# First feed-forward's norm root applied behind PSUM, norm sums in the gap, late latent work of block one spread

## The reference

```python
def first_block(x, ...):
    xn = rmsnorm(x, norm_mix_g)
    # MLA attention (8 heads) over latents of rank 384 and 256, differential attention (4 heads)
    q = rmsnorm(q_lat, mla_q_norm_g) @ mla_w_uq      # 64 plain and 32 rotated columns per head
    kv = rmsnorm(kv_lat, mla_kv_norm_g) @ mla_w_ukv  # keys (uk) and values (uv)
    x = x + merged @ w_out
    hn = rmsnorm(x, norm_ffn_g)                      # the norm that is moved
    hid = silu(hn @ w_ffn_gate) * (hn @ w_ffn_up)
    x = x + hid @ w_ffn_down
    return rmsnorm(x, norm_final_g)

def second_block(x, c, ...):                         # ada: mod = silu(c) @ ada_w + ada_b
    x = x + 0.5 * gate0 * swiglu(modulate(x, norm_g[0], shift0, scale0), ffn1...)
    x = x + gate1 * hybrid_mixer(modulate(x, norm_g[1], shift1, scale1), ...)
    x = x + 0.5 * gate2 * swiglu(modulate(x, norm_g[2], shift2, scale2), ffn2...)
    return x
```

## Time and profile before

| | |
|---|---|
| median of 3 runs | 1987.5 us (1986.34 to 1988.85) |
| profiled execution: time, span | 1989.44 us, 1987.8 us |
| PE busy | 1948.9 us, 98% |
| DVE, ACT, POOL busy | 1007.3, 724.4, 57.6 us |
| mean granted TensorE clock | 0.996 of full speed |

### The profile page before, as it was taken

One profiled execution on the slowest core, in us unless ns is written; L12 is line 12 of the kernel. 1 busy time (PEld: TensorE's weight loads), 2 busy tenths in 40 slices (PEclk: granted clock), 3 DMA queues, 4 the chain that ended last, 5 costly groups with the idle time before them and its releaser, 6 DMA issues.

```text
span 1987.8 us, 25472 instructions
## 1 busy us (share of the span) xinstructions
PE 1948.9 (98%) x9196; PEld 1577.2 (79%) x9200; DVE 1007.3 (51%) x1572; ACT 724.4 (36%) x1225; POOL 57.6 (3%) x95
## 2 busy tenths in 40 slices
PE   9998999999999999999999999999999999999999
PEld 6776777877888888788888887867778878888887
DVE  6757335656655554643334335867834653333322
ACT  5455344432222222422322324445545442223221
POOL 0001000001111000000000001000000000000000
PEclk9999999999999999999999999999999999999999
DMA  5211212227667554333333332211111323333332
GB/s 175 75 64 54 64 54 75 86 73 238 208 216 220 175 191 126 106 107 100 95 95 98 104 106 75 76 64 43 43 54 44 101 69 107 101 97 96 96 106 95
DMA packets 57521, 207.22 MB, mean 104 GB/s; under 512 B 6448, under 2 KB 6576, under 8 KB 57440
## 3 DMA queue, kind: packets, MB, share of 16 engines
q1 hardware_dynamic: 46800, 167.68, 27.0%
q0 software_dynamic: 10640, 38.44, 6.2%
HBM read 203.96 MB, written 2.10 MB: 104 GB/s over the span
## 4 chain that ended last, share of the span: by engine, by line
PE 89%; DVE 5%; ACT 3%; issue 2%; DMA 1%; DVEq 0%; SPq 0%; ACTq 0%; POOLq 0%
PE PS L426 25%; PE PS L428 25%; PE PS L427 25%; PE PS L920 2%; PE PS L889 1%; PE PS L904 1%; DVE Y L1591 1%; DMA ADA<-ada 1%; PE PS L682 1%; ACT HI L1073 1%; PE PS L876 1%; DVE LO L1488 1%; DVE BIAS L1866 1%; PE PS L448 1%; ACT XH L1122 1%
## 5 line engine op out<-in xcount | busy, mean ns | idle before, releaser
L1488 DVE TENSOR_TENSOR LO<-RAW,HI 128x1024 fp32r<-128x1024 f32 x311 | 380.7, 1225 | 462.1 <-ACT HI L1073 461.0
L426 PE MATMUL PS<-XH,HI 128*128 128x512 f32 x1472 | 593.2, 403 | 9.1 <-DVE GATE_1M L1934 3.5
L428 PE MATMUL PS<-XH,LO 128*128 128x512 f32 x1472 | 575.7, 391 | 0.0
L427 PE MATMUL PS<-XL,HI 128*128 128x512 f32 x1472 | 574.9, 391 | 0.0
L1073 ACT ACTIVATE HI<-RAW 128x1024 fp32r<-128x1024 f32 x311 | 328.5, 1058 | 597.5 <-PE PS L428 591.4
L426 PEld LDWEIGHTS PS<-XH,HI 128*128 128x128 f32 x1472 | 277.4, 188 | 77.3 <-issue 20.9
L428 PEld LDWEIGHTS PS<-XH,LO 128*128 128x128 f32 x1472 | 277.0, 188 | 59.2
L427 PEld LDWEIGHTS PS<-XL,HI 128*128 128x128 f32 x1472 | 277.9, 189 | 50.8
L426 PE MATMUL PS<-HIDH,HI 128*128 128x512 f32 x528 | 206.3, 391 | 0.0
L427 PE MATMUL PS<-HIDL,HI 128*128 128x512 f32 x528 | 206.1, 390 | 0.0
L428 PE MATMUL PS<-HIDH,LO 128*128 128x512 f32 x528 | 206.1, 390 | 0.0
(11 more groups left out here) (364 smaller groups left out, 2145.0 us busy)
## 6 DMA issues: line engine op xcount, KB each, us to landing
RAW<-weights SPq DMA_DIRECT2D x311, 512.0 KB, 3.6
ADA<-ada POOLq DMA_DIRECT2D x72, 512.0 KB, 4.6
X<-x_in SPq DMA_DIRECT2D x4, 512.0 KB, 7.4
y_out<-X SPq DMA_DIRECT2D x8, 256.0 KB, 4.5
SQC<-squares SPq DMA_DIRECT2D x1, 320.0 KB, 9.7
TAB_P<-positions POOLq DMA_DIRECT2D x1, 256.0 KB, 4.8
POS<-positions POOLq DMA_DIRECT2D x1, 256.0 KB, 3.5
LAMS<-lambdas POOLq DMA_DIRECT2D x1, 128.0 KB, 5.4
```

Source lines behind the costliest of these rows:

```text
L426: mm(bank, a, moving[0][:, t, :], start=start, stop=False)
L427: mm(bank, a, moving[1][:, t, :], start=False, stop=False)
L428: ins = mm(bank, z, moving[0][:, t, :], start=False, stop=stop)
L1488: V.tensor_tensor(LO[n0 % 3][:], RAW[n0 % 3][:], HI[n0 % 3][:].bitcast(F32), ALU.subtract)\
```

## The change

Four things are changed.

**Norm 3.** ACT and DVE make `XH` and `XL` out of x and the gain alone (`gained`, `gained_lo`), tile by tile during `out_proj(0)`. `behind` starts at once after `out_proj`; the norm's sums stand behind its third tile, the spread behind its sixth. The roots are copied to `R0`. DVE multiplies each gate bank by `R0` (`scale_gate`) before ACT's Silu, which now waits for `gate_scaled`; the up bank stays unscaled, and the down product is multiplied by `R0` before it is added to x.

**Norms 4, 5, 6.** `first_sums` leaves the last product and opens the gap; tile 6's square is added by DVE, so that it sums `RB[:, 0]` (and `SUM_G` for norm 4) only. The last tile of x is added in two halves of 256 tokens, and each half is squared by itself. `WARM` has one or two idle matmuls less in its first place.

**Late latent work.** `piece_step` puts the query product uq0 from step 10 to 11 and uq2 from 11 to 12, KR is rotated at step 11 instead of 13, the placing of queries is divided, and DVE makes half of the key copies (`nope_keys`) that ACT made.

**POOL.** The two memsets of `QF` and `KF` wait for the last product's chunks instead of the last addition to x.

```diff
-WARM = [None, None, None, (2, 1, 1), (2, 2, 1), (2, 1, 1), (2, 1, 1)]
+WARM = [None, None, None, (1, 1, 1), (0, 2, 1), (1, 1, 1), (1, 1, 1)]
...
-    return 2 + p if p < 5 else 7 + (p - 5) // 2 if p < 15 else p - 3
+    return 2 + p if p < 5 else 7 + (p - 5) // 2 if p < 12 else 5 + p // 2 if p < 16 else p - 3
...
-    pool.wait_ge(sem("x_added"), 3 * DT)
+    pool.wait_ge(sem("chunk_used"), FIRST["down2"] + 3 * DT - 2)
     pool.memset(QF[64:66, :, :], 1.0).then_inc(sem("f_ones"), 1)
+    pool.wait_ge(sem("chunk_used"), FIRST["down2"] + 3 * DT - 1)
     pool.memset(KF[64:66, :, :], 1.0).then_inc(sem("f_ones"), 1)
...
+        first_sums(k)
...
-        pe.wait_ge(sem("squared"), NTB[k + 1] - 1)
-        for n, src in enumerate((RB[:, 0, :], SQ[:, 0, :])):
+        for b in range(NB):
+            mm(PS[:, 7, 8 + b:9 + b], RB[:, 0, b * P:(b + 1) * P], SQV["ones"][:, 0:1],
+               start=b == 0, stop=False)
+        if k == 4:
+            pe.wait_ge(sem("g_sum_added"), DT)
             for b in range(NB):
...
-            pe.wait_ge(sem("g_squared"), DT - 1)
-            pe.wait_ge(sem("g_sum_added"), DT - 1)
...
-        pe.wait_ge(sem("squared"), NTB[k + 1])
         for b in range(NB):
+            if b == 0:
...
+            if k == 3 and t == 2:
+                first_sums(3)
+                last_sums(3)
+            if k == 3 and t == 5:
+                norm_spread(3)
...
-            sums = {5: lambda: first_sums((3, 6)[b])} if m == DT - 1 else {}
-            used(split_product(PS[:, m % 4, :], w, range(8), range(8), (mh, ml), between=sums))
+            used(split_product(PS[:, m % 4, :], w, range(8), range(8), (mh, ml)))
...
-        all_released()
+        if f:
+            all_released()
+        else:
+
+            pe.wait_ge(sem("x_added"), XA["out1"] + 6)
...
                 if isinstance(i, int) and i == 0 and j == 0:
                     behind(k, n0, (0, 1))
+                    if f == 0:
+                        all_released()
...
-    norm(3)
...
+        A(SQ[:, 1, 0:S // 2], X[:, nt - 1, 0:S // 2], ACT.Square).then_inc(sem("half_squared"), 1)
+        act.wait_ge(sem("x_added"), XA[AHEAD[k]] + DT)
+        A(SQ[:, 1, S // 2:S], X[:, nt - 1, S // 2:S], ACT.Square).then_inc(sem("squared"), 1)
...
+        if k == 3:
+            return
...
-            for m in range(2 * (p - 18), 2 * (p - 18) + 2):
...
+            m = 2 * (p - 18)
+            act.wait_ge(sem("uk_done"), m + 1)
...
+                if b == 0:
+                    gained(m - 1)
...
+    def gained(t):
+
+        A(XH[:, t, :], X[:, t, :], ACT.Copy, scale=col("g_ffn", t)).then_inc(sem("split_hi"), 1)
...
-                act.wait_ge(sem("chunk_used"), 6 * i + (n0 + 2 * j + 1))
-                A(SILU[j], PS[:, 2 * j, :], ACT.Silu).then_inc(sem("silu"), 1)
+                if f == 0:
+                    act.wait_ge(sem("gate_scaled"), 3 * i + (j + 1))
+                    A(SILU[j], SILU[j], ACT.Silu).then_inc(sem("silu"), 1)
...
+        if k == 3:
+            V.tensor_copy(R0[:], PS[:, 6, :]).then_inc(sem("normed"), 1)
+            v.wait_ge(sem("normed"), NDB[4])
+            return
...
+                .then_inc(sem("q_rotated"), 1)
+
+    def nope_keys(m):
...
+            v.wait_ge(sem("uk_done"), m + 1)
+        for r in range(2):
+            h = 2 * m + r
+            V.tensor_copy(KM[h // 4][0:64, h % 4, :], PS[64 * r:64 * r + 64, latent_bank(f"uk{m}"), :])\
+                .then_inc(sem(LATENT_FREE[f"uk{m}"][0] if r else "key_placed"), 1)
...
-            if s == 13:
+            if s == 11:
                 rotate_shared_keys()
-            if s in (14, 15):
-                rotate_queries(s - 14)
+            if s == 14:
+                turn_queries(0)
+            if s == 15:
+                place_queries(0, range(4))
+            if s in (15, 16):
+                nope_keys(2 * (s - 15) + 1)
...
+            if a == 1 and u == 0:
+                turn_queries(1)
+            if a == 1 and 1 <= u < 3:
+                place_queries(1, range(2 * u - 2, 2 * u))
+            if a == 1 and u == 3:
+                v.wait_ge(sem("q_rotated"), 8)
...
+            if m:
+                add_square(k, m - 1)
+                if b == 0:
+                    gained_lo(m - 1)
...
+            for part in parts(m):
+                x, y = X[:, m, part], PS[:, m % 4, part]
+                if b == 0:
+                    ins = V.tensor_tensor(x, x, y, ALU.add)
...
+    def parts(m):
+
+        return (slice(0, S // 2), slice(S // 2, S)) if m == DT - 1 else (slice(0, S),)
...
+                if f == 0:
+                    scale_gate(i, j)
...
+        def scale_gate(i, j):
+
+            v.wait_ge(sem("chunk_used"), 6 * i + (n0 + 2 * j + 1))
+            V.tensor_tensor(SILU[j], PS[:, 2 * j, :], R0[:], ALU.mult).then_inc(sem("gate_scaled"), 1)
...
+                if f < 2 and not (isinstance(i, int) and (i, j) == (0, 0)):
+                    add_square(4 + f, j - 1, i)
+                    if f == 0:
+                        add_square_g(j - 1, i)
...
+                for part in parts(2 * i + j) if f < 2 and isinstance(i, int) else (slice(0, S),):
+                    y = PS[:, 2 + j:3 + j, part]
+                    x = X[:, bass.ds(2 * i + j, 1), part]
+                    if f == 0:
+                        V.tensor_tensor(T[:, 1:2, part], y, R0[:, part].unsqueeze(1), ALU.mult)\
+                            .then_inc(sem("down_scaled"), 1)
+                        if isinstance(i, int):
+                            v.wait_ge(sem("down_scaled"), 2 * i + j + 1 + (part.stop == S and 2 * i + j == 7))
+                        else:
+                            v.wait_ge(sem("down_scaled"), 2 * i + (j + 1))
+                        ins = V.tensor_tensor(x, x, T[:, 1:2, part], ALU.add)
```

More of the change, by code:

```diff
@@ L888, in attention @@
                             pe.wait_ge(sem("v_copied"), 2 * NB + u + 1)
+                        if a == 1 and u == 4 * NB:
+                            pe.wait_ge(sem("q_rotated"), 8)
+                            pe.wait_ge(sem("k_shared"), 8)
                         mm(PS[:, u % 3, 0:n], at_["q"](h, i), at_["k"](h, n), start=True, stop=False)
@@ L997, in two @@
                                 pe.wait_ge(sem("hid_lo"), FT * f + 8 * g + blocks)
-                            sums = {}
-                            if f < 2 and isinstance(i, int) and (i, j, g) == (3, 1, 1):
-                                sums[4] = lambda: first_sums(4 + f)
                             used(split_product(PS[:, 2 + j, :], w, range(blocks), range(8 * g, 8 * g + blocks),
-                                               (HIDH, HIDL), first=g == 0, last=g == 2, between=sums))
+                                               (HIDH, HIDL), first=g == 0, last=g == 2))
                 two(0)
@@ L1123, in high, with norm @@
                         .then_inc(sem("split_hi"), 1)
-            def norm(k, first=0):
+            def norm(k):
                 nt, src, width, g, oh, ol = NORMS[k]
-                for t in range(first, nt):
-                    square(k, t)
+                act.wait_ge(sem("x_half"), k - 2)
+                act.wait_ge(sem("sum_added"), SAB[k] + nt - 2)
+                A(SQ[:, 1, 0:S // 2], X[:, nt - 1, 0:S // 2], ACT.Square).then_inc(sem("half_squared"), 1)
+                act.wait_ge(sem("x_added"), XA[AHEAD[k]] + DT)
+                A(SQ[:, 1, S // 2:S], X[:, nt - 1, S // 2:S], ACT.Square).then_inc(sem("squared"), 1)
                 stds(k)
@@ L1361, in attention @@
                         k = u - 4
+                        if k == 0:
+                            act.wait_ge(sem("q_rotated"), 8)
                         if k:
@@ L1386, in out_proj @@
                         square(k, m - 1)
+                        if b == 0:
+                            gained(m - 1)
                 load_roots()
-                act.wait_ge(sem("x_added"), XA[f"out{b + 1}"] + DT)
-                norm(k, first=DT - 1)
+                if b == 0:
+                    act.wait_ge(sem("x_added"), XA["out1"] + DT)
+                    gained(DT - 1)
+                norm(k)
+            def gained(t):
+                A(XH[:, t, :], X[:, t, :], ACT.Copy, scale=col("g_ffn", t)).then_inc(sem("split_hi"), 1)
             def ffn(f):
@@ L1440, in ffn @@
                     load_roots()
-                    act.wait_ge(sem("x_added"), XA[f"down{f + 1}"] + DT)
-                    norm(4 + f, first=DT - 1)
+                    norm(4 + f)
             act.wait_ge(sem("eps_set"), 1)
@@ L2096, in two @@
                                 .then_inc(sem("g_last"), 1)
-                        if f < 2 and not (isinstance(i, int) and (i, j) in ((0, 0), (3, 1))):
-                            add_square(4 + f, j - 1, i)
-                            if f == 0:
-                                add_square_g(j - 1, i)
                 two(0)
```

86 lines of the change are left out of this document (43 added, 43 removed).

## The result

The changed kernel takes 1972.4 us (median of four runs, 1969.0 to 1974.0) against 1988.2 us: ratio 0.9916, interval 0.9900 to 0.9933, a gain of 15.8 us where 19.6 were forecast. Two later sets of the same kernel gave 0.9915 (0.9902 to 0.9929) and 0.9901 (0.9887 to 0.9916), 1971.9 and 1969.4 us.

A forecast was written before the change was run, and what follows sets the result against it. PE, busy 98% of the span, was taken as the bound, gaining only from waits, non-product work and lower clock. Gains 5.3 + 6.0 + 0.4 + 3.5 + 2.7 + 1.7 = 19.6 us gave 1968 us, range 1962 to 1974.

The forecast's parts named there:

- two of the rivals: Clock also falls in gaps of norms 5 and 6: near 1971, chance 0.12; late latent work gives little: 1972, chance 0.15.
- A: Late latent work of block one, 138 to 190 us: `OD` and query product waits go, key copy waits remain; 5.3 us gained.
- B: Norm 3, from its first sums to the product behind `behind`: 21.57 us become 15.6, 6.0 us gained if nothing waits.
- the ada term: PE's wait for the first ada accumulator: 0.4 us gained, between -1.4 and +1.
- The ada stall: PE's 2.70 us wait for an ada accumulator: its chain of pieces moves with DVE's progress, 0.4 us gained.
- C: Norm 4: sums leave the last product, clock probably falls again in the gap; 3.5 us gained.
- D and E: Norms 5 and 6: sums leave the product, 1.7 us each; at norm 5 the moved memset gives 1.0 more, 2.7 us.
- the first rival: The clock falls in the gaps of norms 5 and 6 too: 1.6 us each, near 1971; chance 0.12.
- Silu behind DVE: Hidden-tile loop: Silu waits for DVE, `LO` comes late in 22 tiles; no gain, or 1997 us; chance 0.03.

The follow-up runs named there:

- norm3_old: Changed kernel with norm 3 in its gap again, no scaling of gate or down, division into halves kept: 1971.8 us, ratio 0.9915.
- norm3_again: Second set of the changed kernel with norm 3 in its gap again: 1974.4 us, ratio 0.9922, beside 1969.4 for the changed kernel.
- ada_early: Changed kernel with DVE making the first two ada pieces in norm 3, around the roots: 1965.2 us, ratio 0.9886.
- pool_old: Changed kernel with POOL's memsets of `QF` and `KF` behind the last addition to x again: 1971.5 us.
- the last two experiments: Changed kernel with early ada pieces, key copies first, query additions later, idle matmuls back at norm 4: 1960.0 us; the same with norm 3 in its gap: 1962.6 us.

## Why the prediction held, and where a term was off

The time lay in the range and the sign was right. The time alone is no proof of the mechanism, since 1972.4 us is nearer to what two of the rivals gave (1971 and 1972) than to 1968; the stretches tell them apart. By its steps:

- **A** (5.3): right in size, 5.3, 4.3 and 6.6. The three differ as the clock does: it was at half for 6.8, 10.2 and 3.4 us here. The wait for ACT's key copy was forecast at 3.2 us and is 3.2; DVE's was 2.9 at full clock and is 1.9: uk2's matmuls ran at half clock and fill more of the time, and uk3 starts 4.5 us behind uk2 (175.75 and 171.28), where 4.3 were worked out. The 0.4 us for slow time at uk3 was too little in the first trace: the clock is 0.57 over the 8 us from 171.
- **B** (6.0): the stretch was forecast at 15.6 us and is 15.25. Of the gain, 2.4 to 2.7 us come with the sums' place and the halves, not with the norm's move, as `norm3_old` and `norm3_again` show; the prediction did not part the two. The `LO` wait at the first odd chunk is 0.7, 0.3 and 0.8 us in the three traces (0.25 before), inside the bound of the ada term and not in its value.
- **The ada stall** (0.4 gained): the mis-sized term. The wait itself is 2.9, 2.3 and 2.3 us in the three traces, which is near the 2.3 implied. What follows it was not in the sum: in two of three traces the clock stays down for 3.4 us more, 1.6 us lost. "The chain moves with it" was right for this order of DVE's list, and `ada_early` shows that another order frees the chain from it.
- **C** (3.5): right, 3.1 to 3.4, with the fall of the clock in gap 4 in all of the changed kernel's traces. Two counts were given in matmuls where passes were meant: the insertion at norm 4 is 32 passes and that at norms 5 and 6 is 16; the times used were the rows' own.
- **D and E** (2.7, 1.7): right, 2.8 and 1.9. The clock did not fall in these gaps in the changed kernel's three traces, so the first rival is out for it. The margin is small: in `pool_old` it falls at norm 5, behind one wait of 1.18 us more.
- **Silu behind DVE**: from the second to the eighth ada sum the two kernels run in step within 0.03 us, so `scale_gate` costs nothing in the loop, as costed.
- **Left out altogether**: the stretch before 138 us, which no edit touches, ran from 1.9 us ahead to 1.4 us behind. In the first trace the clock was 0.51 from 117 to 124 us.
- **The range**: the bounds given add up to about 5.0 us downwards and 3.2 upwards as a root sum square, not to 4.5 both ways.

The spread between the changed kernel's own traces is in good part the lower clock. Windows of one microsecond over the whole span but its last 3 us, each counted by what its granted clock lacks of 1.00, and doubled, give the time at half clock: 17 us before, 24 us in the changed kernel's first trace, 24 in the second, 14 in the third, 3.4 in each of the last two experiments. Between the first and the third that is 10 us, of which half is lost, 5 us; the spans are 1972.3 and 1967.0. The first and the second, with the same 24 us, are 2.2 us apart: by the table it lies at the ada sum (1.6 us) and in A and B. What makes a given stretch come or not at 95, 118 and 170 us in kernels with the same work there stays open. The division of the last tile into halves was not tried by itself.

## What to carry to other kernels

When an engine is nearly full, price a change by the stalls it closes, and then ask what stands next in the same list: here the waits for `OD` went, but the wait for ACT's key copy stayed and one for DVE's came, and the wait at the ada sum stayed in every version until its chain was started in a gap. Spans of two kernels that differ by a few us say little while slow stretches come and go; compare the start of one and the same instruction at the bounds of stages. A gap in which the root's chain is awaited anyway takes short sums for nothing, but at norm 4 the idle matmuls that they displaced had been holding the clock.

## What the runs showed of the hardware

The granted clock falls behind one-column sums and behind waits, and the same code does not always meet it: from 116 to 125 us its mean is 0.62, 0.81 and 1.00 in the three traces of one kernel. With two idle matmuls between the sums of norm 4 it stays at 1.00 (three traces of three), without them it was 0.57 for 4 us, and it fell in nine traces of nine. A memset of 3.5 us on POOL makes DVE's copy of 128x256 take 1.54 us instead of 0.29, ending 0.15 us behind the memset, and leaves a subtraction of two SBUF operands of 128x1024 at 1.23 us.
